# Prompt attention scores: even and odd heads issued in turn instead of one after the other

## The reference

```python
h = rmsnorm_mod(x, norm1_g, sh1, sc1)
qkv, u, v, ga, gb = in_projection(h, w_in)
# per group g, per head, blocks of 128 queries against the block before and their own:
scores = einsum('bnqrhd,bnkrhd->bnrhqk', qb, kc) * 64 ** -0.5
scores = where(valid, scores - slope * dist, -inf)
m = max(scores); p = exp(scores - m); den = sum(p); o = einsum(p, vc) / den
# the three groups are combined per head with weights proportional to exp(log-sum-exp)
x = x + gate1 * ((ga * (A @ w_pa) + gb * (B @ w_pb)) @ w_o)
x = x + gate2 * HierMoE(rmsnorm_mod(x, ...))      # 16 experts, top 2
```

## Time and profile before

| | |
|---|---|
| median of 3 runs | 1329.01 us (1328.84 to 1329.03) |
| span of the profiled execution, first to last instruction | 1324.4 us |
| around the span (median less span; the profiled execution has no total of its own) | 4.6 us |
| PE busy | 1241.9 us, 94% |
| matmul records of L1159 | 240, in three stretches: 363.9 to 378.5, 492.9 to 505.1 and 610.1 to 622.3 us |

### The profile page before, as it was taken

How to read it: one execution, slowest core, us unless ns; L and a number is a source line. 1 busy time by engine, 2 the same in 40 slices (tenths; PEclk the granted TensorE clock), 3 DMA queues, 4 the chain that set the end, 5 groups by cost and what they waited for, 6 DMA issues and landing times. The chain is left out here.

```text
span 1324.4 us, 17978 instructions
## 1 busy us (share of the span) xinstructions
PE 1241.9 (94%) x7160; PEld 942.6 (71%) x7160; DVE 660.8 (50%) x920; ACT 546.3 (41%) x878; POOL 194.4 (15%) x228
## 2 busy tenths in 40 slices
PE   4899999999999999998799999999999999999987
PEld 1677877776788877886665666747757888778762
DVE  1328513223061214123466542254687888888877
ACT  3723313011372135215333333211346877777752
POOL 1203200010000010001200001100035322222220
PEclk9999999999999999999799999999989999999999
DMA  9642211263524453539679996811299999999973
GB/s 359 222 189 96 72 64 64 65 231 128 199 105 136 147 190 112 170 134 339 230 276 347 348 366 182 307 37 69 92 327 292 357 373 374 373 375 374 366 283 111
DMA packets 126235, 293.96 MB, mean 222 GB/s; under 512 B 10160, under 2 KB 10288, under 8 KB 121496
## 3 DMA queue, kind: packets, MB, share of 16 engines
q1 hardware_dynamic: 108216, 243.57, 52.2%
q0 software_dynamic: 17952, 49.44, 10.5%
HBM read 269.91 MB, written 30.42 MB: 227 GB/s over the span
## 5 line engine op out<-in xcount | busy, mean ns | idle before, releaser
L982 PE MATMUL psum<-part,part 128*128 128x512 f32 (+1 forms) x1088 | 441.5, 406 | 10.3 <-DVE part L1924 5.0
L983 PE MATMUL psum<-part,part 128*128 128x512 f32 (+1 forms) x1088 | 429.1, 394 | 0.0
L984 PE MATMUL psum<-part,part 128*128 128x512 f32 (+1 forms) x1088 | 429.0, 394 | 0.0
L982 PEld LDWEIGHTS psum<-part,part 128*128 128x128 f32 (+1 forms) x1088 | 227.2, 209 | 71.4 <-issue 21.8
L984 PEld LDWEIGHTS psum<-part,part 128*128 128x128 f32 (+1 forms) x1088 | 227.1, 209 | 40.2
L983 PEld LDWEIGHTS psum<-part,part 128*128 128x128 f32 (+1 forms) x1088 | 228.0, 210 | 35.9
L2342 DVE TENSOR_TENSOR part<-arena,part 128x2048 fp32r<-128x2048 f32 x96 | 219.0, 2290 | 35.0 <-ACT part L1774 33.9
L1873 DVE TENSOR_TENSOR part<-arena,part 128x2048 fp32r<-128x2048 f32 x42 | 96.3, 2301 | 252.6 <-PE psum L1024 226.3
L1774 ACT ACTIVATE part<-arena 128x2048 fp32r<-128x2048 f32 x94 | 179.7, 1920 | 44.8 <-DMA arena<-in_w_up_dram 22.5
L1546 ACT ACTIVATE arena<-psum 128x512 f32<-128x512 f32 (+3 forms) x140 | 75.7, 567 | 247.0 <-PE psum L984 202.1
L970 PE MATMUL psum<-cst,arena 128*128 128x128 f32 (+2 forms) x858 | 122.5, 283 | 40.3 <-DMA cst<-in_consts_dram 12.8
(11 more groups left out here) (289 smaller groups left out, 1075.0 us busy)
## 6 DMA issues: line engine op xcount, KB each, us to landing
arena<-in_w_in_dram SPq DMA_DIRECT2D x34, 1024.0 KB, 5.4
arena<-in_cache_kv_w_dram SPq DMA_DIRECT2D x16, 2048.0 KB, 11.8
arena<-in_w_gate_dram SPq DMA_DIRECT2D x32, 1024.0 KB, 9.9
arena<-in_w_up_dram SPq DMA_DIRECT2D x32, 1024.0 KB, 9.9
arena<-in_w_down_dram SPq DMA_DIRECT2D x32, 1024.0 KB, 9.8
arena<-in_w_ada_dram SPq DMA_DIRECT2D x24, 1024.0 KB, 7.6
arena<-in_cache_kv_w_dram SPq DMA_DIRECT2D x16, 1024.0 KB, 9.1
arena<-in_w_ada_final_dram SPq DMA_DIRECT2D x8, 1024.0 KB, 7.7
```

The costliest lines, as they stand in the source:

```text
L982: nc.tensor.matmul(out_, hi, w_hi, start=start, stop=False)
L983: nc.tensor.matmul(out_, hi, w_lo, start=False, stop=False)
L984: last_product[0] = nc.tensor.matmul(out_, lo, w_hi, start=False, stop=stop)
```

## The change

The two loops over heads are exchanged. Before, all four even heads of a key tile go into one bank, then all four odd heads into the next. After, the heads alternate: even head 0, odd head 0, even head 1, and so on, in the two halves of the rows and into two banks. PE waits for both banks before the first of the eight matmuls, and the two `mm_filled` rises come with the last even and the last odd matmul. The numbering of the banks and every other list stay as they are.

```diff
                 for kk, kt in enumerate(keys):
+                    m = mm.first[f"s{g}{i}"] + 2 * kk
                     for par in range(2):
-                        m = mm.first[f"s{g}{i}"] + 2 * kk + par
-                        mm.wait_empty(pe, m)
-                        for j in range(4):
-                            ins = nc.tensor.matmul(mm.bank(m)[:, j * P:(j + 1) * P],
+                        mm.wait_empty(pe, m + par)
+                    for j in range(4):
+                        for par in range(2):
+                            ins = nc.tensor.matmul(mm.bank(m + par)[:, j * P:(j + 1) * P],
                                                    qT[64 * par:64 * par + 64, j, i * P:(i + 1) * P],
                                                    kT[64 * par:64 * par + 64, j, kt * P:(kt + 1) * P],
                                                    start=True, stop=True)
-                        ins.then_inc(mm_filled, 1)
+                            if j == 3:
+                                ins.then_inc(mm_filled, 1)
```

## The result

The changed kernel is **slower**: median 1332.84 us (13 runs) against 1328.56 us of before (13 runs), ratio 1.0036, 95% interval 1.0022 to 1.005. The forecast was 1327.2, the range ended at 1330.8.

What follows compares the result with a forecast made beforehand. PE, busy 94% of a 1324.4 us span, was taken as the bound. Of 6.4 us off its list 4.6 became waits; 1.7 + 0.1 + 0 = 1.8 us saved gave 1329.01 - 1.8 = 1327.2, range 1324.4 to 1330.8.

Steps and rivals of the forecast that it cites:

- The steps and the stretches: Score stretches on PE: 16, 32, 48 records become 8, 16, 24 steps, taking 6.4 us off PE's list.
- the overlap of three records in eight: Scores before the change: three of a bank's eight records already run beside the other half, leaving 5 paid steps a bank.
- Group 0: First group of score tiles: 1.7 us saved of 2.6, the rest lost to waits for ACT and DVE.
- The wait for DVE's bank at tile 3: Group 0: the last pair of tile 3's scores waits for bank four until 375.65 us.
- Groups 1 and 2, the waits: Before tile 0's transposes: the wait for ACT's exponentials grows from 0.84 to about 2.2 us.
- the rival's price: Clock falls in group 1 or 2's longer wait: one fall costs 2.1 us, giving 1329.3; chance 0.17.
- both falls: Clock falls in the waits of both groups 1 and 2: costs 4.2 us, giving 1331.4; chance 0.08.
- the 1.8 us of the sum: Whole kernel: saving of 1.7 in group 0, 0.1 in group 1 and 0 in group 2, carried whole to the end.
- The clock gives something back: Group 2's end: the low clock falls elsewhere, saving a further 2.6 us, giving 1324.6; chance 0.10.
- The 4.6 us "around the span": Time outside the profiled execution's span, added to 1322.6 us to reach 1327.2.

Runs made afterwards that it cites:

- two-and-two order: The changed kernel with heads in the order even, even, odd, odd, still two banks at once; one execution, 1333.86 us.
- work moved: The changed kernel with each group's second ada_step moved behind the scores of tile 2; 1330.39 us, ratio 1.0024 to the kernel before.
- groups 1 and 2 alone: Heads alternate only in groups 1 and 2, group 0 as in the kernel before; 1331.26 us, ratio 1.0028.
- group 2's end at full clock: The kernel before with useless matmuls in group 2: one before tile 2's exponentials, two before tile 3's; 1325.10 us, ratio 0.9991.
- two useless matmuls: The changed kernel with two useless float32 matmuls before tile 0's exponentials in groups 1 and 2; 1323.78 us, ratio 0.9977.
- moved work: The kernel before, without alternation, with group 1's two ada_steps put ahead of the scores of tile 0; 1336.13 us, ratio 1.0066.
- group 0 alone: Heads alternate only in group 0, groups 1 and 2 as in the kernel before; 1324.78 us, ratio 0.998.
- one filler: The changed kernel with exponentials signalled in halves and one useless matmul before tile 0's transposes in groups 1 and 2; 1322.34 us, ratio 0.9956.

## Why the prediction was wrong

**The steps and the stretches: right.** 3.26, 2.06 and 1.16 us were foreseen as "about 3.1", 2.03 and 1.14. The two halves run side by side, and the overlap of three records in eight that the argument started from is what the two-and-two order shows again.

**Group 0: right to 0.1 us.** The wait for DVE's bank at tile 3 is there. At tile 0 the last exponential (370.56 us) allows the transposes at 371.09, and PE came to them just then, at 371.10, so no wait for ACT is left to see. The group was measured alone at 0.998, whose interval holds the forecast 0.9987.

**Groups 1 and 2, the waits: right.** 2.15 us for "about 2.2", ending as long after the first score as before.

**The step that failed is the rival's price and with it its chance.** The prediction said of a fall in the longer wait: "2.1 to 2.6 us in all", "One such fall in group 1 or 2 costs 2.1", and for both falls 1331.4. The mechanism was named, at the right place. But the price counted the low clock over one set of transposes and values alone. It lasted 17 us in group 1, and everything up to the transposes of tile 2 was under it. From the rows: values 0 and 1 take 3.65 for 1.97, the scores of tile 3 2.08 for 1.16, the transposes 1.97 for 1.09, the samples product 3.68 for 1.95. With the transposes of tiles 0 and 2, which were low in part, that is 8.0 us more. Three waits of 0.34 for ACT's copies vanish in it, and the scores of tile 3 would have won 0.55 at full clock; 6.4 is left against before. Group 2's fall cost 3.6 in this execution, so there the two were 10.0 us, not 4.2. Between the medians they come to about 6.1 (the 4.3 us lost and the 1.8 us of the sum), an estimate that takes the rest of the sum as right. The loss of group 1, from its scores to those of group 2 and against 117.18, goes with the length of its low stretch: 2.4 us for 7 (work moved), 3.3 for 10 (groups 1 and 2 alone), 5.3 for 14 (two and two) and 6.4 for 17. So 2.1 was about the price of the shortest fall. The length could have been read ahead: the low clock that was already in the trace of before lasted 17 us and did not end with the next busy stretch either,

```profile
628.50:645.50 17.00, 14.96 (x66) 13.88 (x67) 6.62 (x18) 6.27 (x24) 5.29 (x8) 0.50 0.30 93
```

and I had put it down as a state of group 2's end and not as the length of a fall.

**The chance.** I gave the falls 0.25 together, though PE was to be idle in that wait for longer than it was where the clock had fallen already. The profile had both numbers (1.49 us idle and a fall, 2.2 us to come), and the comparison should have made the rival the likeliest case.

**"The clock gives something back", 2.6 us:** not what happened, since the fall moved forward and did not go away. Its size is left about as it was: with group 2's end at full clock 2.4 us arrived at the sample attention in one profile, and the ratio, 0.9991, can tell it neither from 2.6 us nor from nothing.

**The 4.6 us "around the span"** were wrong (1.6 to 1.8 everywhere on record), but the forecast did not hang on them: it is the same against the median.

Shown by experiments: the fall follows from idle time and not from alternation (two useless matmuls remove it, moved work brings it about without alternation), and it is the whole loss (0.9977 and 0.9972 with the clock up, against 0.998 for group 0 alone). Left open: why the low stretch of group 1 lasts about 7 us in one kernel, 10 or 14 in others and 17 in a third, since each was profiled once and no run separated this from the spread between executions. Open too is why a long wait brings a fall in one execution and not in another: PE waits 2.33 us ahead of the L982 matmul at 1290.61 us and ahead of the same one at 1282.20 before, and the clock fell only in the first.

## What to carry to other kernels

Before making PE's work denser, look at what it waits for next. If it is another engine on a fixed schedule, all that is won becomes idle time, and idle time in a stretch of small matmuls can take the clock down for many times its own length. Price such a fall over everything that stands behind it until the trace has the clock back. Then cut the wait itself (here by signalling half of the result early, 0.9946, or 0.9956 with one filler), or fill it (0.9972 and 0.9977), and alternating row halves is worth having.

## What the runs showed of the hardware

The granted clock stayed at 0.50 for 17 us through a stretch in which PE was busy for 16.97 of 17.00 us: small float32 matmuls and transposes that follow each other without a gap did not bring it back. In group 1 the clock fell in all six profiles in which PE waited 1.49 us or more for tile 0's exponentials (once in two pieces, 0.61 and 0.88; otherwise 1.95 to 3.22), and in none of the eight in which it waited 1.09 or less. And two row halves in two banks run at the speed of one: 32 records take 2.06 us, and the 16 steps of one half alone come to 0.24 + 16 x 0.112 = 2.03.
